# Two value passes a head instead of three, value halves moved into the attentions, and four tiles at once in an output projection

## Chip, cores and metric

The kernel runs on one core of one Trainium2 chip. The metric is the device time of one execution in microseconds; before the change three runs had a median of 1339.58 us (1339.01 to 1339.7).

## What is computed

Two transformer blocks over 512 tokens of width 1024, one after the other, in float32. Of the reference only the three attentions and what surrounds them matters here:

```
# block 1
h = rms_norm(x, mix_norm_g);  proj = h @ w_in
fq, fk, fv, flog, dq, dk, dv = split(proj)         # 512 columns each (flog: 8)
fox_out  = softmax(q k^T/8 + cumulated log gates, causal) v       # "fox": 8 heads of 64
diff_out = rms_norm((softmax(q1 k1^T/8 + alibi) - lam softmax(q2 k2^T/8 + alibi)) v)  # "diff": 4 heads, v is 128 wide
x = x + concat(fox_out, diff_out) @ w_out
x = x + (silu(h w_gate) * (h w_up)) @ w_down;  x = rms_norm(x)
# block 2
q, k, v, c_a, c_b, g_a, g_b = split(rms_norm(x) @ w_in_2 + b_in_2)
br_a = neighbourhood_attention(q, k, v, rpb) @ w_na_out           # "na": 8 heads of 64
br_b = silu(layer_norm(dwconv31(c_a * sigmoid(c_b)))) @ w_conv_out
x = x + (sigmoid(g_a) * br_a + sigmoid(g_b) * br_b) @ w_out_2
x = x + (gelu(gate) * val) @ w_down_2;  out = rms_norm(x)
```

## The kernel before, in words

**Precision.** Every operand is split into a high part (what the tensor engine's fp32r format keeps) and a low part (the rest). A product is three matmuls into one PSUM bank: high x high, high x low, low x high (`mm3`, L764 to L766).

**Weights.** They come in units of 128 x 1024 floats, numbered in the order of use by `plan_units`. SyncE loads unit u into one of two RAW buffers (L608) once GpSimd has made the low part of unit u-2. ScalarE converts RAW to the high part WH (`hi_part`, L1214; four slots, so it waits until unit u-4 is used), GpSimd subtracts to the low part WL (L736). `hi_next(u)` converts unit u+4 and stands in ScalarE's program where unit u has just been used. SyncE's list also holds the copies that put a head's rows in place (`head_rows`, L617 to L620); `HEADS_BEFORE` says ahead of which unit. They wait for ScalarE's split of that head (`head_part`, L1277 or L1279, semaphore head_hi).

**Attention.** Each of the three attentions is a list of 32 score tiles (128 queries against up to 512 keys), run in steps 0 to 36 that all engines walk through in the same order. In step i TensorE does: the scores of tile i (L945, L946); filler, which is chunks of projections taken from `fill_plan`; the value pass for the probabilities of tile i-4 (`pv_half`, for every second tile; for "diff" `pv`, once a head); the transposes of tile i-2 (L960). ScalarE does: the copy PTH of the transposed tile i-3 (L1361), the exponential of tile i (L1371), the scaling of tile i-1 (L1378), the copy of a finished head's output (L1401), then the splits of heads that `HEAD_STEPS` lists for this step, then `hi_next` for the filler that ends in this step. VectorE does: mask, minimum and negation of tile i (L1949), the reciprocal, low parts of heads (L1792, L1795), other work (`behind`: mask steps in "fox", taps of the convolution in "na", L2135), the low part PTL (L1983), the output's low part (L2001, L2004), and draining of the fillers. A value pass waits for PTL (ptl_done). In step 4h+8 head h's output is drained.

**Values.** `pv_half` uses as stationary operand the 128 value columns of a pair of heads (L764 to L766 with PTH, PTL) and takes half of the output rows. The four value tiles of each half of a projection (`v_tile`, `v_phase`, `v_parts`) are computed ahead of the attention: eight tiles ahead of "fox" (v1) and of "na" (v3). VectorE drains a tile with one scaling to T (L1746 with a bias row BVB, L1749), ScalarE copies T to VH, VectorE subtracts to VL (L1755).

**Output projection.** `half_units("out1", ...)` multiplies the "diff" half of the mixed heads. Its first two tiles take chunk k as soon as diff head k is ready (`mixed_ready`), the last of which is normalised and split after the last step (`diff_normed(3)`, `diff_low(3)`, L1908, L1913).

**Convolution.** `tap_plan` spreads 124 taps: 48 ahead of "na", 38 in its steps, 38 later.

Of the kernel before, what the change touches and what calls it, by code (L numbers as in the profile page):

```python
# [33 lines left out]
F32 = mybir.dt.float32  # L34
# [28 lines left out]
def plan_units():  # L63
# [28 lines left out]
    for j in range(4):  # L92
        u += col("w_in_2", NQ + P * j) + col("w_in_2", NK + P * j)
        if j == 0:
            u += v("w_in_2", NV)
# [40 lines left out]
def program(nc, d):  # L136
# [40 lines left out]
    def heads_memory(tag, o):  # L177
        return dict(VH=at("VH" + tag, o, [P, TC, S], F32R), VL=at("VL" + tag, o + 8192, [P, TC, S], F32R),
# [24 lines left out]
    BVB = at("BVB", BIG + 82432, [P, S], F32)  # L203
# [20 lines left out]
    CAUSAL = at("CAUSAL", BIG + 84480, [P, S], F32)  # L224
    NMB = tiny("NMB", [P, 2, S], BF16)
# [38 lines left out]
    def tap_plan():  # L264

        early = [(t, 0) for t in range(6)]
        for t in range(21):
            early += [(t, 1), (t + 6, 0)]
        during = []
        for t in range(4):  # L270
            during += [(t + 21, 1), (t, 2), (t + 27, 0), (t, 3)]
        for t in range(4, 10):
            during += [(t + 21, 1), (t, 2), (t, 3)]
        for t in range(10, 12):
            during += [(t, 2), (t, 3)]
# [26 lines left out]
    bv_in = sem("bv_in")  # L302
# [60 lines left out]
    o_free = sem("o_free")  # L363
    od_copy = sem("od_copy")
# [36 lines left out]
    for name, n in [("init", 8), ("fox0", 2), ("v1", 8), ("foxf", 8), ("v2", 4), ("difff", 18), ("out1", 8),  # L401
                    ("ffn1", 44), ("down1", 8), ("cab", 8), ("na0", 2), ("v3", 8), ("naf", 6), ("gates_b", 8),
# [4 lines left out]
    UN = {"fox0": 0, "v1": 2, "foxf": 6, "v2": 14, "difff": 16, "out1": 28, "ffn1": marks["ffn1"],  # L407
          "down1": marks["down1"], "cab": marks["down1"] + 24, "na0": marks["down1"] + 32,
          "v3": marks["down1"] + 34, "naf": marks["down1"] + 38, "gates_b": marks["gates"], "gates_a": marks["gates"] + 8,
          "na_out": marks["na_out"], "conv_out": marks["na_out"] + 4, "out2": marks["na_out"] + 8,  # L410
          "ffn2": marks["ffn2"], "down2": marks["down2"]}
    assert UN["out1"] + 4 == UN["ffn1"] and UN["naf"] + 6 == UN["gates_b"]
# [3 lines left out]
    for name in TL:  # L416
        PT0[name] = n_part
        n_part += {"init": 8, "v": 6, "v2": 3, "difff": 7, "out1": 4, "na_out": 4, "conv_out": 4}.get("v" if name in ("v1", "v3") else name, 0)


    per = {"init": (8, 8), "v1": (8, 8), "fox0": (0, 0), "foxf": (0, 0), "v2": (4, 4), "difff": (4, 0),
# [339 lines left out]
    def _(pe):  # L761
# [149 lines left out]
        for i in range(1, 4):  # L911
            v_tile("v1", i)
# [1437 lines left out]
```

## Time and profile before

| | before |
|---|---|
| median of 3 runs | 1339.58 us |
| profiled execution | 1337.46 us |
| its span (first to last instruction) | 1335.6 us |
| granted TensorE clock | 0.998 |
| POOL (GpSimd) busy | 670.1 us |
| ACT (ScalarE) busy | 639.8 us |

The page's busy time of PE (TensorE) counts a matmul from its start to its modelled end, and matmuls overlap. The distance between two starts tells what a matmul costs. A number in square brackets behind a row of an engine's order of time is the idle time before the instruction, and what ended it. An idle time on an engine other than the one that bounds costs nothing by itself.

### The profile page before, as it was taken

The numbers are of one execution on the slowest core, as the hardware profiler recorded it, in microseconds if no ns is written. First come the engines' busy times: TensorE is split into PE (matmuls) and PEld (weight loads), VectorE is DVE, ScalarE is ACT, GpSimd is POOL, SyncE is SP. The second block draws the span as 40 slices with busy tenths as digits, with TensorE's granted clock in tenths as the row PEclk, the third lists the DMA queues.
The fourth block names the chain that finished last, engine by engine and source line by source line (L and its number), as shares of the span: only waits on it lengthen the run. The fifth ranks groups of instructions, "written<-read, shape, count | busy, mean of one in ns | idle before, by whom it ended". The sixth has DMA issues, their size and how long they took to land.

```text
span 1335.6 us, 19126 instructions
## 1 busy us (share of the span) xinstructions
PE 1315.9 (99%) x6457; PEld 1104.4 (83%) x6457; DVE 657.5 (49%) x1237; ACT 639.8 (48%) x1015; POOL 670.1 (50%) x884
## 2 busy tenths in 40 slices
PE   9999999999999999999999999999999999999998
PEld 7988878788888888888888888888888888888887
DVE  7576586742222221112698884867445555551112
ACT  4488576754444333333436874464454444442222
POOL 7432343446555554555465344555655555554550
PEclk9999999999999999999999999999999999999999
DMA  6332332223333333333463332322333333333331
GB/s 181 99 85 72 80 111 80 64 79 111 101 102 95 94 102 93 92 103 92 93 144 92 82 82 77 94 95 80 110 93 97 100 101 97 94 90 101 89 99 63
DMA packets 220333, 127.22 MB, mean 95 GB/s; under 512 B 8642, under 2 KB 215887, under 8 KB 220143
## 3 DMA queue, kind: packets, MB, share of 16 engines
q1 hardware_dynamic: 220247, 126.39, 33.5%
q8 instruction: 37, 0.61, 0.2%
q14 instruction: 25, 0.20, 0.0%
q10 hardware_dynamic: 24, 0.01, 0.0%
HBM read 117.56 MB, written 2.47 MB: 90 GB/s over the span
## 4 chain that ended last, share of the span: by engine, by line
PE 90%; DVE 3%; ACT 3%; issue 2%; DMA 1%; POOL 1%; DVEq 0%; POOLq 0%; ACTq 0%
PE PS L764 28%; PE PS L766 28%; PE PS L765 28%; PE PS L960 1%; DMA RAW<-in_w_in 1%; PE PS L945 1%; PE PS L946 1%; ACT WH L1214 1%; POOL WL L736 1%; PE PS L841 0%; DVE PTL L1983 0%; DVE PS L2135 0%; PE PS L1159 0%; DVE PR L1949 0%; PE PS L867 0%
## 5 line engine op out<-in xcount | busy, mean ns | idle before, releaser
L736 POOL TENSOR_TENSOR WL<-RAW,WH 128x256 fp32r<-128x256 f32 x864 | 662.5, 798 | 635.3 <-ACT WH L1214 635.1
L1214 ACT ACTIVATE WH<-RAW 128x1024 fp32r<-128x1024 f32 (+1 forms) x220 | 228.8, 1042 | 436.0 <-PE PS L766 374.9
L764 PE MATMUL PS<-XH,WH 128*128 128x512 f32 x1072 | 419.1, 391 | 0.0
L765 PE MATMUL PS<-XL,WH 128*128 128x512 f32 x1072 | 417.8, 390 | 0.0
L766 PE MATMUL PS<-XH,WL 128*128 128x512 f32 x1072 | 417.8, 390 | 0.0
L766 PEld LDWEIGHTS PS<-XH,WL 128*128 128x128 f32 x1072 | 201.2, 188 | 42.7
L765 PEld LDWEIGHTS PS<-XL,WH 128*128 128x128 f32 x1072 | 201.3, 188 | 40.1 <-issue 0.7
L764 PEld LDWEIGHTS PS<-XH,WH 128*128 128x128 f32 x1072 | 201.3, 188 | 40.0 <-issue 0.7
L764 PE MATMUL PS<-HH,WH 128*128 128x512 f32 (+1 forms) x374 | 141.0, 377 | 0.0
L766 PE MATMUL PS<-HH,WL 128*128 128x512 f32 (+1 forms) x374 | 140.8, 377 | 0.0
L765 PE MATMUL PS<-HL,WH 128*128 128x512 f32 (+1 forms) x374 | 140.8, 377 | 0.0
L2071 DVE TENSOR_TENSOR T<-PS,R 128x512 f32<-128x512 f32 x44 | 30.3, 691 | 167.8 <-PE PS L766 158.2
L765 PEld LDWEIGHTS PS<-HL,WH 128*128 128x128 f32 x374 | 70.4, 188 | 13.0
L764 PEld LDWEIGHTS PS<-HH,WH 128*128 128x128 f32 x374 | 70.4, 188 | 13.0
L766 PEld LDWEIGHTS PS<-HH,WL 128*128 128x128 f32 x374 | 70.4, 188 | 12.7
L2263 DVE TENSOR_TENSOR T<-PS,R 128x512 f32<-128x512 f32 x44 | 30.4, 691 | 65.8 <-PE PS L766 56.2
L1371 ACT ACTIVATE PR<-PR,NM 128x384 f32<-128x384 f32 (+2 forms) x88 | 49.7, 565 | 26.7 <-DVE NM L1949 25.7
L764 PE MATMUL PS<-WH,XH 128*128 128x256 f32 x192 | 54.8, 285 | 1.2 <-DVE T L1746 1.2
L765 PE MATMUL PS<-WL,XH 128*128 128x256 f32 x192 | 54.3, 283 | 0.0
L766 PE MATMUL PS<-WH,XL 128*128 128x256 f32 x192 | 54.3, 283 | 0.0
L2094 DVE TENSOR_TENSOR X<-PS,X 128x512 f32<-128x512 f32 x8 | 5.5, 692 | 98.0 <-PE PS L766 98.0
L2135 DVE SCALAR_TENSOR_TENSOR PS<-U,VEC,PS 128x512 f32<-128x512 f32 x78 | 53.6, 748 | 0.1
(335 smaller groups left out, 1865.1 us busy)
## 6 DMA issues: line engine op xcount, KB each, us to landing
RAW<-in_w_up SPq DMA_DIRECT2D x66, 512.0 KB, 3.7
RAW<-in_w_in SPq DMA_DIRECT2D x60, 512.0 KB, 3.9
RAW<-in_w_down SPq DMA_DIRECT2D x32, 512.0 KB, 3.7
RAW<-in_w_gate SPq DMA_DIRECT2D x22, 512.0 KB, 3.7
RAW<-in_w_out SPq DMA_DIRECT2D x16, 512.0 KB, 3.6
RAW<-in_w_down SPq DMA_DIRECT2D x16, 384.0 KB, 3.2
QB<-QA SPq DMA_DIRECT2D x24, 128.0 KB
KA<-KA SPq DMA_DIRECT2D x24, 128.0 KB
```

What stands on the lines that cost most here:

```text
L736: ins = pool.tensor_tensor(WL[:, s, cs], RAW[:, s % 2, cs], WH[:, s, cs].bitcast(F32), ALU.subtract)
L764: pe.matmul(out, ah, bh, start=start, stop=False)
L765: pe.matmul(out, ah, bl, start=False, stop=False)
L766: return pe.matmul(out, al, bh, start=False, stop=stop)
L945: pe.matmul(out, mem["QA"][:, e, q], mem["KA"][:, e, ks], start=True, stop=False)
L946: pe.matmul(out, mem["QB"][:, e, q], mem["KB"][:, e, ks], start=False, stop=True).then_inc(sc_ready, 1)
L960: ins = pe.transpose(PS[:, TRB + g % 2, k * P:(k + 1) * P], probs[:, k * P:(k + 1) * P], IDF[:, :])
L1214: act.activation(WH[:, s, 0:width], RAW[:, s % 2, 0:width], ACT.Copy).then_inc(w_hi, 1)
L1371: act.activation(probs, probs, ACT.Exp, scale=-1.0, bias=NM[:, g % 4:g % 4 + 1], accum_out=RS[:, g % 4:g % 4 + 1]).then_inc(exp_ready, 1)
L2071: dve.tensor_tensor(T[:, s, 4:4 + S], src, R[:, :], ALU.mult).then_inc(acc_free, 1)
L2135: dve.scalar_tensor_tensor(out=homes[k], in0=src, scalar=w, in1=homes[before], op0=ALU.mult, op1=ALU.add).then_inc(conv_done, 1)
L2263: dve.tensor_tensor(T[:, s, 4:4 + S], src, R[:, :], ALU.mult).then_inc(acc_free, 1)
```

## The change

1. `pv_half`: the stationary operand is one head's 64 high and 64 low value columns side by side (V, a view of the memory of VH and VL), with two matmuls per key block (against PTH and PTL) instead of three. The result's two halves of 64 rows are added: ScalarE copies one (o_half), VectorE adds the other in PSUM (o_sum), for "na" with the bias, which makes the bias row BVB needless; then the output is copied and split as before. "diff" keeps its three matmuls.
2. Second value halves of "fox" and "na" become filler at steps 12 to 17 and 14 to 17; the Q tile of pair 1 of "fox" moves ahead of the attention; other fillers are respaced; the last value tile for "diff" becomes filler too. A value tile is now drained from PSUM by ScalarE (v_hi), then by VectorE (v_lo).
3. The unit order puts the second half of the values in front of the K tile of pair 3; the places of the head rows in the load list follow.
4. `tap_plan`: 40 taps ahead of "na", 46 within.
5. out1: two pairs of tiles run chunks 0 to 2 before the wait for diff head 3.

```diff
@@ plan_units
-    u += v("w_in", FOX_V)
+    u += v("w_in", FOX_V)[:2]
     for j in range(1, 4):
-        u += col("w_in", FOX_Q + P * j) + col("w_in", FOX_K + P * j)
+        u += col("w_in", FOX_Q + P * j)
+        if j == 3:
+            u += v("w_in", FOX_V)[2:]
+        u += col("w_in", FOX_K + P * j)
...
@@ units and fillers
-    UN = {"fox0": 0, "v1": 2, "foxf": 6, "v2": 14, "difff": 16, "out1": 28, "ffn1": marks["ffn1"],
+    UN = {"fox0": 0, "v1": 2, "foxf": 4, "v2": 14, "difff": 16, "out1": 28, "ffn1": marks["ffn1"],
...
-        qk_steps = [(0, 2), (3, 5)] + [(4 * f - 2, 4 * f + 1) for f in range(2, 8)]
         if kind == "fox":
-            for f in range(8):
-                add("qk", f, a + f, u + f, *qk_steps[f])
-            for i in range(3):
-                add("v", i, TL["v2"] + i, UN["v2"], N_SCORES + i, N_SCORES + i, False, PT0["v2"] + i + 1)
+            order = [("qk", 1, 0, 2), ("qk", 2, 3, 5), ("qk", 3, 6, 8), ("qk", 4, 9, 11), ("v", 0, 12, 13), ("v", 1, 14, 14),
+                     ("v", 2, 15, 16), ("v", 3, 17, 17), ("qk", 5, 18, 21), ("qk", 6, 22, 25), ("qk", 7, 26, 29)]
+            a, u = a + 1, u + 1
         elif kind == "na":
-            for f in range(6):
-                add("qk", f, a + f, u + f, *qk_steps[f])
-            for c in range(KD):
-                s0 = N_SCORES - 10 + 2 * c
-                add("gb", c, TL["gates_b"] + c, UN["gates_b"] + c, s0, min(s0 + 1, LAST_STEP))
+            order = [("qk", 0, 0, 2), ("qk", 1, 3, 5), ("qk", 2, 6, 8), ("qk", 3, 9, 11), ("qk", 4, 12, 13), ("v", 0, 14, 14),
+                     ("v", 1, 15, 15), ("v", 2, 16, 16), ("v", 3, 17, 17), ("qk", 5, 18, 20)]
...
+        if kind == "fox":
+            for i in range(TC):
+                add("v2", i, TL["v2"] + i, UN["v2"], N_SCORES - 2 + 2 * i, min(N_SCORES - 1 + 2 * i, LAST_STEP), i == 3,
+                    PT0["v2"] + i + 1)
+        elif kind == "na":
+            for c in range(KD):
+                s0 = N_SCORES - 11 + 2 * c
+                add("gb", c, TL["gates_b"] + c, UN["gates_b"] + c, s0, s0 + 1)
...
@@ SyncE's list
-    for kind, first in (("fox", UN["foxf"] + 6), ("diff", UN["difff"] + 6), ("na", UN["naf"] + 6)):
+    for kind, first in (("fox", UN["foxf"] + 7), ("diff", UN["difff"] + 6), ("na", UN["naf"] + 7)):
         for i, head in enumerate(range(2, 8)):
-            later = 1 if kind == "diff" else 0
+            later = 1 if kind == "diff" or kind == "na" and head >= 6 else 0
             HEADS_BEFORE.setdefault(first + i + later, []).append((kind, head))
...
@@ TensorE: pv_half
-                vc = slice((hd // 2) * P, (hd // 2) * P + P)
+                if half == 0 and hd == 4:
+                    pe.wait_ge(acc_free, late_values(kind))
+                values = mem["V"][:, :, hd, :, :].rearrange("p t a b -> p t (a b)")
...
                 for kc in kcs:
-                    ins = mm3(PS[:, OB + g % 2, q], mem["VH"][:, kc, vc], mem["VL"][:, kc, vc],
-                              mem["PTH"][:, kc, q], mem["PTL"][:, kc, q], kc == kcs[0], kc == kcs[-1])
+                    pe.matmul(PS[:, OB + g % 2, q], values[:, kc, :], mem["PTH"][:, kc, q], start=kc == kcs[0], stop=False)
+                    ins = pe.matmul(PS[:, OB + g % 2, q], values[:, kc, :], mem["PTL"][:, kc, q], start=False,
+                                    stop=kc == kcs[-1])
...
@@ TensorE: out1
+        pe.wait_ge(w_lo, UN["out1"] + 1)
+        for k in range(3):
+            mixed_ready(k)
+            out1_tiles([0], [k])
+        pe.wait_ge(w_lo, UN["out1"] + 2)
+        pe.wait_ge(acc_free, TL["out1"])
+        out1_tiles([1], range(3))
+        mixed_ready(3)
+        out1_tiles([0, 1], [3])
...
@@ ScalarE, VectorE: a head's output
+                if kind != "diff" and i - 5 in ready_after and ready_after[i - 5] % 4 == 3:
+                    hd = ready_after[i - 5] // 4
+                    own, other = half_rows(hd % 2), half_rows(1 - hd % 2)
+                    act.wait_ge(pv_ready, o0 + hd + 1)
+                    act.activation(o_temp(kind)[own, :], PS[other, OB + (o0 + hd) % 2, :], ACT.Copy).then_inc(o_half, 1)
...
+                    dve.wait_ge(o_half, f["o1"] + hd + 1)
+                    if kind == "fox":
+                        dve.tensor_tensor(bank[own, :], bank[own, :], o_temp(kind)[own, :], ALU.add).then_inc(o_sum, 1)
...
@@ ScalarE, ahead of "na"
-        v_parts("v3", M2, bias_columns)
+        act.wait_ge(rt_ready, 1)
+        for i in range(TC):
+            bias_columns(2 * i)
+            bias_columns(2 * i + 1)
+            v_hi("na", first_values("v3", i))
+        act.activation(LAM[:, 6:7], BT[:, :], ACT.Exp)
...
@@ VectorE, taps in "na"
-        attention("na", RP[:, :], lambda i: conv_taps(2 if N_SCORES - 8 <= i < N_SCORES else int(i % 4 != 3), n_during))
+        attention("na", RP[:, :], lambda i: conv_taps(2 if N_SCORES - 8 <= i <= N_SCORES else 1, n_during))
```

## Rows read from the trace of the kernel before

**Rows 1.** The page, busy us (share of the span) and instructions.
```profile
PE 1315.9 (99%) x6457; PEld 1104.4 (83%) x6457; DVE 657.5 (49%) x1237; ACT 639.8 (48%) x1015; POOL 670.1 (50%) x884
```

**Rows 2.** Stretches: length, busy us (instructions) PE, PEld, DVE, ACT, POOL; clock; DMA.
```profile
56.85:152.13 95.28, 92.84 (x578) 82.10 (x577) 61.57 (x180) 71.35 (x164) 30.42 (x40) 1.00 0.31 79
...
107.00:130.00 23.00, 23.00 (x142) 20.36 (x141) 13.43 (x44) 18.74 (x45) 6.69 (x10) 1.00 0.28 70
...
780.34:795.77 15.43, 15.43 (x87) 13.34 (x86) 14.27 (x29) 10.28 (x22) 7.26 (x8) 1.00 0.35 91
```

**Rows 3.** TensorE in order of time: start us, us; filler, then a value pass.
```profile
117.15 0.39 PE L766 MATMUL PS<-XH,WL 128*128 128x512 f32 x1
117.38 0.28 PE L764 MATMUL PS<-PTH,VH 128*128 128x256 f32 x1
117.50 0.28 PE L765 MATMUL PS<-PTL,VH 128*128 128x256 f32 x1
117.62 0.28 PE L766 MATMUL PS<-PTH,VL 128*128 128x256 f32 x1
```

**Rows 4.** TensorE in order of time, where it waited (and one transpose, 791.25).
```profile
68.58 0.55 PE L960 MATMUL PS<-IDF,PR 128*128 128x128 f32 x3 [0.74 <-ACT PR L1378]
...
76.99 0.39 PE L764 MATMUL PS<-PTH,VH 128*128 128x256 f32 x1 [0.70 <-DVE PTL L1983]
...
135.95 0.39 PE L764 MATMUL PS<-PTH,VH 128*128 128x256 f32 x1 [1.00 <-DVE PTL L1983]
...
170.91 0.36 PE L945 MATMUL PS<-KA,QA 128*128 128x256 f32 x1 [1.27 <-issue]
...
255.01 0.47 PE L764 MATMUL PS<-MH,WH 128*128 128x512 f32 x1 [1.98 <-DVE ML L1913]
...
696.49 0.36 PE L764 MATMUL PS<-WH,XH 128*128 128x256 f32 x1 [1.24 <-DVE T L1746]
...
734.95 0.39 PE L764 MATMUL PS<-PTH,VH 128*128 128x256 f32 x1 [1.07 <-DVE PTL L1983]
...
791.25 0.38 PE L960 MATMUL PS<-IDF,PR 128*128 128x128 f32 x2
```

**Rows 5.** ScalarE in order of time.
```profile
110.86 0.59 ACT L1401 ACTIVATE MH<-PS 64x512 fp32r<-64x512 f32 x1
...
114.87 1.04 ACT L1214 ACTIVATE WH<-RAW 128x1024 fp32r<-128x1024 f32 x1
115.82 0.57 ACT L1361 ACTIVATE PTH<-PS 128x512 fp32r<-128x512 f32 x1
...
696.37 0.53 ACT L1505 ACTIVATE BN<-BNR 128x384 f32<-128x384 f32 x1 [0.99 <-DVE T L1746]
696.80 0.40 ACT L1261 ACTIVATE VH<-T 128x256 fp32r<-128x256 f32 x1
...
789.49 1.06 ACT L1214 ACTIVATE WH<-RAW 128x1024 fp32r<-128x1024 f32 x1 [3.27 <-DMA RAW<-in_w_in]
```

**Rows 6.** VectorE in order of time; the last row is the page's, all taps.
```profile
111.49 0.69 DVE L2001 TENSOR_TENSOR ML<-PS,MH 64x512 fp32r<-64x512 f32 x1 [1.40 <-ACT MH L1401]
...
116.43 0.69 DVE L1983 TENSOR_TENSOR PTL<-PS,PTH 128x512 fp32r<-128x512 f32 x1
...
805.34 1.23 DVE L2135 SCALAR_TENSOR_TENSOR SQ<-U,VEC,SQ 128x512 f32<-128x512 f32 x1
...
L2135 DVE SCALAR_TENSOR_TENSOR PS<-U,VEC,PS 128x512 f32<-128x512 f32 x78 | 53.6, 748 | 0.1
```

**Rows 7.** SyncE's issues in order of time: start us, us, line, what.
```profile
116.43 0.57 SPq L608 DMA_DIRECT2D RAW<-in_w_in  x1
...
123.79 0.59 SPq L608 DMA_DIRECT2D RAW<-in_w_in  x1
...
168.52 0.60 SPq L620 DMA_DIRECT2D KA<-KA  x1
```

**Rows 8.** The page, DMA issues: count, KB each, us from issue to landing.
```profile
RAW<-in_w_in SPq DMA_DIRECT2D x60, 512.0 KB, 3.9
```

More of the change, by code:

```diff
@@ L494, in values_due, with values_place, values_shape, first_values @@
     def values_due(kind, step):
-        return [it for it in fill_plan(kind) if kind == "diff" and it["what"] == "v" and it["s1"] == step - 1]
+        return [it for it in fill_plan(kind) if it["what"] == "v" and it["s1"] == step - 1]
+    def values_place(kind, t, half):
+        mem = FAM[kind]["mem"]
+        if kind == "diff":
+            c = slice(256 * half, 256 * half + 256)
+            return mem["VH"][:, t, c], mem["VL"][:, t, c]
+        return tuple(mem["V"][:, t, 4 * half:4 * half + 4, j, :] for j in range(2))
+    def values_shape(kind, ap):
+        return ap if kind == "diff" else ap.rearrange("p (h c) -> p h c", c=HD)
+    def first_values(name, i):
+        return dict(what="first", idx=i, a=TL[name] + i, unit=UN[name], part=PT0[name] + i + 1)
+    def late_values(kind):
+        return max(it["a"] for it in fill_plan(kind) if it["what"] == "v") + 1
     def fill_chunks(it, step, n):
@@ L525, in keys_of, with o_temp @@
         return NA_KEYS[qb] if kind == "na" else (0, qb + 1)
+    def o_temp(kind):
+        return OTN if kind == "na" else ODR[:, 0, :]
     def pair_index(kind, hd):
@@ L537, in head_tiles @@
         if pair == 0:
-            a = {"fox": TL["fox0"], "diff": TL["foxf"] + 6, "na": TL["na0"]}[kind]
+            a = {"fox": TL["fox0"], "diff": TL["foxf"] + 10, "na": TL["na0"]}[kind]
             return a, a + 1
+        if kind == "fox" and pair == 1:
+            return TL["foxf"], TL["foxf"] + 1
         return tuple(it["a"] for it in fill_plan(kind) if it["what"] == "qk" and it["idx"] in (2 * pair - 2, 2 * pair - 1))
@@ L910, in _ @@
         ins.then_inc(fl_ps, 1)
-        for i in range(1, 4):
+        for i in range(1, TC):
             v_tile("v1", i)
@@ L920, in _ @@
         ins.then_inc(cum_ps, 1)
-        for i in range(4, 8):
-            v_tile("v1", i)
+        fm_tile(UN["foxf"] // 4, UN["foxf"] % 4, TL["foxf"])
         def attention(kind):
@@ L1128, in _ @@
         rt_transposes(RP)
-        for i in range(8):
+        for i in range(TC):
             v_tile("v3", i)
@@ L1307, in gate_logs @@
                     act.dma_start(dst, src).then_inc(head_in[head], 16)
-        v_parts("v1", M1, gate_logs)
+        act.wait_ge(rstd_tokens, 1)
+        for i in range(TC):
+            gate_logs(i)
+            v_hi("fox", first_values("v1", i))
+        gate_logs(TC)
+        act.activation(LAM[:, 6:7], BT[:, :], ACT.Exp)
+        hi_next(UN["foxf"])
         def gate_part(c):
@@ L1756, in v_low, with v_lo, v_phase @@
                               ALU.subtract).then_inc(low_done, 1)
-        def v_phase(name, mem, bias, extra):
-            slots_drained(name)
-            for i in range(8 + 1):
-                if i < 8:
-                    v_take(name, i, bias)
-                if i >= 1:
-                    v_low(name, i - 1, mem)
+        def v_lo(kind, it, name):
+            t, half = it["idx"], int(it["what"] == "v")
+            hi, lo = values_place(kind, t, half)
+            dve.wait_ge(act_done, H0[name] + t + 1)
+            dve.scalar_tensor_tensor(out=lo, in0=values_shape(kind, ps(it["a"], 256)), scalar=RT[:, t:t + 1],
+                                     in1=hi.bitcast(F32), op0=ALU.mult, op1=ALU.subtract).then_inc(acc_free, 1)
+        def v_phase(kind, name, extra):
+            for i in range(TC):
+                v_lo(kind, first_values(name, i), name)
                 extra(i)
+            extra(TC)
         def qk_take(name, i, r):
```

170 lines of the change are left out of this document (85 added, 85 removed).

## The prediction, made before the changed kernel was run

> **What bounds the kernel now.** I read the page first, then the busy times of each stage, then TensorE's own order of time, and last what the other engines do at the few places where TensorE stands still. TensorE is busy for 1315.9 of 1335.6 us, VectorE for 657.5 [rows 1]. The engine works through its matmuls in the order in which they are written, so there are only two ways to shorten this kernel: fewer matmuls, or fewer places at which one of them waits. The stage view and the engine's waits say where such places are: 2.4 us of the 95.3 of the first attention ("fox"), 1.2 in the third value projection, 1.1 and some small ones in the third attention ("na"), 2.0 before the output projection [rows 2, 4]. The last steps of "na" have no wait, but VectorE is busy for 14.27 of 15.43 us in four of them, so they have the least room [rows 2].
>
> A step is one score tile; three things then follow in each step: filler (projection chunks), the value pass of an earlier step, transposes. ScalarE and VectorE handle the softmax of the same steps, in an order that is also written out.
>
> **Part 1: two value passes instead of three.** The price of a matmul is the distance between two starts, not its listed duration, which overlaps the next one. Value matmuls of 256 columns start 0.12 us apart, though each is listed with 0.28; filler matmuls of 512 columns start 0.23 apart [rows 3]. Now the stationary operand holds a head's high and low half side by side (64+64 columns) instead of two heads' high halves, so high and low need one pass each over the two parts of the probabilities: 2 matmuls for 3. Per head there are 2+4 key blocks in "fox" and 3+3 in "na": 6 x 16 heads = 96 key blocks, so 96 matmuls go. "diff" keeps its three. 96 x 0.12 = **-11.5 us**, all of it on the engine that bounds. (The listed 0.282 each would give 27.1; that is the mistake to avoid.)
>
> The Trainium skill, "TensorE: Matmul & The Clock Gate", section "Wait — 56ns, not 53.3ns?", gives the spacing of warm matmuls as columns / 2.4 GHz plus about 2.5 ns. By that page the estimate is 109 ns at 256 columns and the saving 10.5 us; this trace has 120 ns at a granted clock of 1.00 (2.4 GHz) [rows 2, 3], and the trace decides.
>
> **Part 2: what each head gets in return.** The two halves must be added: ScalarE copies 64 rows from PSUM (0.59 by the nearest row, the copy of the head's output), VectorE adds them (0.69), and only then comes ScalarE's old copy [rows 5, 6]. ScalarE's old copy used to wait for VectorE's queue no longer than for its own; the new handoff runs parallel to ScalarE's exponential and scaling. 16 heads, 1.3 us each, none of it on TensorE. Around steps 20 to 28 ScalarE is busy for 18.74 of 23 us, 8.2 of each 10.08 that a head takes [rows 2]; one more copy makes that 8.8 of 9.4. I book nothing for it in "fox". In the last steps of "na" VectorE's 14.27 plus 0.7 stand against 15.43 - 0.72 for TensorE: 0.3 over, in each of two such stretches, **+0.7** [rows 2].
>
> **Part 3: second value halves as filler.** 4 tiles x 24 matmuls x 0.12 = 11.5 us leave the phase ahead of "fox" and the one ahead of "na" and come back inside; one Q tile (24 x 0.228 = 5.5) goes the other way. The sum on TensorE is zero. What can change is cover. Taken away: the stall of 0.74 (0.90 with the pipeline's refill) at 68.6, behind a late conversion, as units 8 and 9 no longer wait for the second value half; the 1.0 (1.17) at 135.95, as two steps that had no filler now have some; about half of the 0.70 (0.86) at 76.99 [rows 4]: **-2.5**. In "na" TensorE waits 1.07 at 734.95 and 1.1 in small pieces [rows 4]; steps get 0.5 to 1.2 us longer there and the extra convolution taps (0.75 each [rows 6]) take back a part: **-1.4**. Added: the first value tile ahead of "na" is now drained by ScalarE, then VectorE, and ScalarE does two bias columns (0.53 listed, 0.43 to the next start) before it. TensorE waited 1.24 there for VectorE's one operation; the chain is longer by 2 x 0.43 + 0.4 = **+1.2** [rows 4, 5]. The end of "fox" had value tiles of 2.9 us in steps 32 to 34; now 1.4 in each of 30 to 35, so the last value pass finds less ahead of it: between 0 and 2, I take **+1.2**, and 0.2 for the value tiles' own draining. The first scores of "fox" come six us sooner; their key rows are then issued at about 47.9 and, at the 2.4 us from a copy's issue at 168.52 to the scores that waited for it at 170.91 [rows 4, 7], are there at 50.3, before the 50.8 at which they are wanted: nothing.
>
> **Part 4: the output projection.** Before, two tiles run three chunks and wait for the fourth head: 1.98 idle, 2.14 with the refill [rows 4]. Three chunks of two more tiles (18 x 0.228 = 4.1 us) now stand there; their weights are made ready during "diff". Nothing else is late next: **-2.1**.
>
> **Part 5: what is moved in the load queue.** This decides. SyncE issues weights and the heads' rows in one list. The rows of a head wait for ScalarE's split of that head, and every weight load behind them waits too. Before, the fox heads' rows stood ahead of units 12 to 17, now ahead of units 11 to 16; but V[2:] was pushed in front of K3, so unit 15 is no longer the one converted at step 21 with a load issued five steps before: it is still converted at step 21 (four after K3, unit 11), and its load now stands behind head 6, which ScalarE splits in that very step. ScalarE comes to the conversion and waits; its queue is in order, so the probabilities behind it wait, and TensorE's value pass waits for those. In times of the trace before: head 6 split by 114.9, the load behind it issued at 116.43, 3.9 to landing [rows 8] = 120.3, conversion 0.95, transposed copy 0.5, VectorE's low part 0.7: 122.5. TensorE wants it at 117.38, less 0.24 saved since step 20: **+5.3**. Before, the conversion started at 114.87, at once, the low part ended at 117.1, and the pass had only 0.3 us to spare [rows 3, 5 to 7]. Head 7: rows ahead of unit 16, converted at step 25, one step after the split. The load behind its rows was issued at 123.79 [rows 7]; +3.9 + 0.95 + 0.5 + 0.7 = 129.8. TensorE's pass came a period of 10.08 after 117.38, at 127.5, less 0.5 saved in it: **+2.9**. Head 5: ahead of unit 14, converted two steps after the split. Two periods earlier than head 7 the load went out at 103.6, landed at 107.5; steps 16 and 17 now hold a half and a whole value tile (6.0 us instead of 4.7), so conversion, copy and low part end at 109.7 and the pass is due at some 108.6: **+1.1**. "na" has the like once: head 7 ahead of the fifth unit after, its conversion at step 24 instead of 25. Before, ScalarE stood still for 3.27 us there, until the landing at 789.49, and TensorE did not notice, as a whole step of work had gone ahead [rows 5]. Now that step is behind the wait, and the split itself waits for the new addition, behind two taps (up to 1.23 each [rows 6], so +2.4): landing at 791.9, then 0.95 + 0.4 + 0.6 + 0.6 = 794.4 for the scaled probabilities; the transposes that need them stood at 791.25, less 0.36 [rows 4]: 3.5. Without the delay of the split 1.1. I take **+3.0**.
>
> **Sum.** -11.5 - 2.5 - 1.4 - 2.1 = -17.5. Against it 5.3 + 2.9 + 1.1 + 3.0 + 1.2 + 1.2 + 0.2 + 0.7 = +15.6. Net -1.9 us on the profiled execution (1337.5, of which 1335.6 is the span), so 1335.6. The runs' median is 1339.6, 2.1 above the profiled one; I carry the difference over: **1337.7**. Unknown costs at their bounds: head 5 from 0 to 2, end of "fox" 0 to 2, "na" 1.1 to 4, start of "na" 0 to 2, gains inside "na" 0 to 2.3: about 1333 to 1342 for this case.
>
> **Rivals.** (B) The conversions do not hold the softmax up: the loads land earlier than I read, or the pipeline has more steps in hand than the 0.3 and 1.2 us I count. For it: in "na" a block of 3.27 us cost TensorE nothing [rows 5]. Against it: that one had a whole step ahead of it. Then 12.3 us of my debit fall away: 1325.4; half of it, 1331.5.
> (C) The ring of the new handoff, the slower side. Place: step 4h+8 of each head in "fox" and "na". ScalarE copies, VectorE adds, ScalarE copies again, VectorE subtracts; VectorE already stands 1.40 us in that step [rows 6]. If ScalarE has to wait for the addition before the next transposed copy, the bubble is up to 0.6 per head, 16 x 0.6 = 9.6: 1347. It decides from some 0.3 per head, 5 us, on. Against it: the addition (PTL's end, 0.4, plus 0.7) ends with ScalarE's exponential and scaling (1.0 to 1.1). The Trainium skill speaks for (C) in "na": "GPSIMD Engine Reference", section "1. Specifications", says that VectorE and GpSimd contend when VectorE has two SBUF inputs; the convolution taps do, eight more of them move into this attention, and here they take 0.75 on the mean and 1.23 at worst [rows 6].
> (D) The change does not do what it says for the time: the pass is a third shorter, but the pass before the next low part then stands waiting, and half of the 11.5 us turns up again as waits on PTL: 1337.7 + 5.8 = 1343.5. For it: three of the waits shown are on PTL; against it, they sum to 2.8 us only [rows 4], and the steps are not shorter but longer where value tiles and denser filler come in.
>
> **How the numbers follow.** My case 0.48, B 0.31, C 0.12, D 0.09. A measurement of this kernel can tell about 0.2% (2.7 us) from no change, so "same" is 1336.9 to 1342.3. My case falls 0.19 faster, 0.22 same, 0.07 slower, as its own width lies across the lower edge; B is 0.28 faster, 0.03 same; C 0.09 slower, 0.03 same; D 0.05 and 0.04. Together 0.47, 0.32, 0.21. The range takes in most of B and all of D: 1326 to 1344.
>
> **What would show it.** The value matmuls of L764's helper vanish for "fox" and "na" and 192 in two new lines stand there, 0.12 apart. ScalarE's conversion line waits on RAW for some 4 to 5.5 us once near step 21 of "fox", less near steps 18 and 25, and 5 us near step 24 of "na"; TensorE has as many waits on PTL or PR, 5 us the longest. No wait on ML before the output projection. If TensorE's longest wait in "fox" is under 2 us, part 5 is wrong and B holds; if its waits are many and alike, one per head, it is C.

## The result and the profile after

The change makes the kernel slower: 1347.44 us (median of 4, 1346.83 to 1348.34) against 1339.64 for the kernel before, measured beside it (4 runs, 1339.01 to 1341.02). The ratio is 1.0057, its 95% interval 1.004 to 1.0075: +7.8 us, where -1.9 was forecast, and above the stated range (1326 to 1344 us). The profiled execution's span went from 1335.6 to 1345.0, +9.4; the account below explains that difference.

The page of the kernel after: the busy times, the granted TensorE clock in 40 slices, and the weight loads with the median time from issue to landing.

```profile
PE 1311.0 (97%) x6361; PEld 1098.8 (82%) x6361; DVE 664.5 (49%) x1237; ACT 649.6 (48%) x1033; POOL 674.2 (50%) x884
...
PEclk9998899999999999999999999999999999999999
...
RAW<-in_w_in SPq DMA_DIRECT2D x60, 512.0 KB, 4.1
```

Against [rows 1] TensorE has 96 matmuls and 4.9 us of listed busy time less, and yet the span is longer. The fourth and fifth slices, in "fox", show a lower clock, where the kernel before has 9 in all 40. The five largest groups of TensorE's waits from the first scores on (engine, tile, line, releaser: us in total, times, longest):

```profile
PE PS L1010 <- DVE PTL L2047: 12.6, 5, 6.6
PE PS L995 <- ACT PR L1437: 4.4, 2, 4.2
PE PS L800 <- DVE V L1821: 3.6, 2, 2.9
PE PS L980 <- issue: 1.6, 1, 1.6
PE PS L995 <- DVE PTL L2047: 1.2, 1, 1.2
```

L1010 is the new value pass. Four of its five waits in order of time (start, duration, idle before it in brackets):

```profile
105.35 0.39 PE L1010 MATMUL PS<-PTH,V 128*128 128x256 f32 x1 [1.41 <-DVE PTL L2047]
121.57 0.58 PE L1010 MATMUL PS<-PTH,V 128*128 128x256 f32 x1 [6.64 <-DVE PTL L2047]
135.71 0.58 PE L1010 MATMUL PS<-PTH,V 128*128 128x256 f32 x1 [3.19 <-DVE PTL L2047]
155.70 0.39 PE L1010 MATMUL PS<-PTH,V 128*128 128x256 f32 x1 [0.87 <-DVE PTL L2047]
```

These are the places of the prediction's heads 5, 6 and 7 and the end of "fox". The wait on ML ahead of the output projection (1.98 in [rows 4]) is gone. The releaser of the long ones is not where they begin. SyncE's queue (L656 and L657 move a head's rows, L645 is the weight load behind them), and ScalarE's:

```profile
114.56 0.60 SPq L657 DMA_DIRECT2D KA<-KA  x1
115.58 0.38 SPq L645 DMA_DIRECT2D RAW<-in_w_in  x1
...
128.33 0.59 SPq L657 DMA_DIRECT2D KA<-KA  x1
128.97 1.33 SPq L645 DMA_DIRECT2D RAW<-in_w_in  x2
```

```profile
113.39 0.62 ACT L1338 ACTIVATE KA<-T 64x512 fp32r<-64x512 f32 x1
119.25 1.06 ACT L1272 ACTIVATE WH<-RAW 128x1024 fp32r<-128x1024 f32 x1 [5.24 <-DMA RAW<-in_w_in]
120.21 0.58 ACT L1420 ACTIVATE PTH<-PS 128x512 fp32r<-128x512 f32 x1
...
133.40 1.06 ACT L1272 ACTIVATE WH<-RAW 128x1024 fp32r<-128x1024 f32 x1 [4.19 <-DMA RAW<-in_w_in]
...
801.55 1.06 ACT L1272 ACTIVATE WH<-RAW 128x1024 fp32r<-128x1024 f32 x1 [5.35 <-DMA RAW<-in_w_in]
```

Read them as a chain: ScalarE ends the split of head 6 at 114.0, only then may SyncE move its rows and issue the load at 115.58; ScalarE meanwhile stands at the conversion L1272 for 5.24 us until it lands; the probabilities' copy (L1420) is queued behind it, and TensorE's value pass behind that. Something the prediction did not have is in the busy times of the same stretches (window: length, PE, PEld, DVE, ACT, POOL busy, then the granted clock):

```profile
103.56:114.54 10.98, 9.57 (x55) 8.06 (x54) 7.25 (x22) 8.60 (x21) 3.06 (x5) 1.00 0.01 3
114.54:121.50 6.96, 0.39 (x2) 0.00 (x0) 1.05 (x3) 2.25 (x5) 1.12 (x2) 0.73 0.43 115
121.50:132.10 10.60, 10.53 (x53) 9.39 (x54) 6.45 (x21) 7.00 (x17) 1.68 (x3) 0.86 0.25 61
132.10:135.70 3.60, 0.42 (x2) 0.00 (x0) 0.73 (x2) 2.31 (x5) 1.09 (x2) 0.87 0.71 185
135.70:144.00 8.30, 8.29 (x36) 7.36 (x37) 4.46 (x15) 6.29 (x16) 1.71 (x3) 0.64 0.01 3
803.80:810.00 6.20, 5.97 (x27) 5.18 (x28) 6.13 (x13) 4.22 (x11) 6.20 (x7) 0.73 0.30 85
```

The second and fourth are the stalls; behind them TensorE is busy all the time at a mean clock of 0.86 and 0.64, that is, partly at 1.2 instead of 2.4 GHz. There a filler matmul takes 0.43 us to the next start, where [rows 3] has 0.23:

```profile
138.44 0.63 PE L800 MATMUL PS<-XH,WH 128*128 128x512 f32 x1
138.87 0.63 PE L801 MATMUL PS<-XL,WH 128*128 128x512 f32 x1
139.30 0.63 PE L802 MATMUL PS<-XH,WL 128*128 128x512 f32 x1
```

**The account.** From TensorE's order of time, each matmul's distance to the next start is split in three: the usual distance for its width (0.109, 0.120, 0.175 and 0.227 us at 128, 256, 384 and 512 columns); what exceeds it where the next one waited ("stalls"); what exceeds it elsewhere ("slow"). Microseconds, before to after:

| stretch | matmuls | stalls | slow |
|---|---|---|---|
| ahead of fox | 50.6 to 44.5 | 1.4 to 1.4 | 2.8 to 2.6 |
| fox | 91.4 to 91.7 | 2.9 to 13.5 | 1.0 to 5.3 |
| diff to the start of na | 550.9 to 539.4 | 6.6 to 6.4 | 4.3 to 5.6 |
| na to the end | 609.4 to 615.3 | 5.1 to 8.9 | 2.5 to 3.7 |
| difference | -11.4 | +14.1 | +6.6 |

The sum is +9.3 of the +9.4. The matmuls are as forecast. The forecast's other terms made +9.6 of stalls and nothing slow. The growth of "slow" is the clock: of the 5.3 us in "fox", 4.25 fall where the trace grants half the clock (117.7 to 124.5 and 134.8 to 141.6), and the kernel before has no such stretch until its last 6 us.

### The profile page after: what moved, and what is told of

Its sections match the earlier page's. It is cut to its first block, busy times and chain, and to the rows that moved or that the text cites. A ratio compares the mean times of both kernels' runs of the same rounds, so it can differ in the third digit from the quotient of the medians.

```text
span 1345.0 us, 18926 instructions
## 1 busy us (share of the span) xinstructions
PE 1311.0 (97%) x6361; PEld 1098.8 (82%) x6361; DVE 664.5 (49%) x1237; ACT 649.6 (48%) x1033; POOL 674.2 (50%) x884
## 4 chain that ended last, share of the span: by engine, by line
PE 87%; DVE 6%; issue 2%; ACT 2%; DMA 2%; SPq 0%; POOL 0%; DVEq 0%; ACTq 0%; POOLq 0%
PE PS L800 27%; PE PS L801 27%; PE PS L802 27%; DMA RAW<-in_w_in 2%; DVE PS L2201 1%; PE PS L995 1%; PE PS L1010 1%; PE PS L980 1%; PE PS L981 1%; PE PS L1011 1%; DVE PTL L2047 1%; PE PS L877 0%; ACT PTH L1420 0%; DVE SQ L2201 0%; PE PS L1217 0%
## 5 line engine op out<-in xcount | busy, mean ns | idle before, releaser
L1272 ACT ACTIVATE WH<-RAW 128x1024 fp32r<-128x1024 f32 (+1 forms) x220 | 229.4, 1044 | 451.1 <-PE PS L802 368.8
L2341 DVE SCALAR_TENSOR_TENSOR PS<-T,VEC,PS 128x512 f32<-128x512 f32 x44 | 33.3, 756 | 41.3 <-ACT PS L1630 41.3
```

Source lines behind the costliest of these rows:

```text
L1272: act.activation(WH[:, s, 0:width], RAW[:, s % 2, 0:width], ACT.Copy).then_inc(w_hi, 1)
L2341: dve.scalar_tensor_tensor(out=z, in0=T[:, s, 3:3 + S], scalar=w(0), in1=z, op0=ALU.mult, op1=ALU.add).then_inc(cz_tap, 1)
```

## The experiments

"Repaired" below is the kernel after with both edits of the first two experiments. Each group of runs was measured beside the kernel before, whose median moved between groups from 1338.3 to 1339.8. Ratios are to that, with 95% intervals. A difference between two medians of different groups is therefore uncertain by some 1.5 us.

**One: the rows of "fox" a unit later.**

```diff
-    for kind, first in (("fox", UN["foxf"] + 7), ("diff", UN["difff"] + 6), ("na", UN["naf"] + 7)):
+    for kind, first in (("fox", UN["foxf"] + 8), ("diff", UN["difff"] + 6), ("na", UN["naf"] + 7)):
```

> The kernel after, with the rows of heads 2 to 7 of fox one unit later in the load queue (ahead of units 12 to 17 instead of 11 to 16); nothing else. Theory Q (a conversion on ScalarE is stuck behind a load that stands behind the rows of a head that was split just before): the three stalls of fox that follow a wait of ScalarE on RAW (1.57, 6.80 and 3.35 us over the pitch) go, 11.7 us, and with them the 4 us in which matmuls of fox ran at twice their distance after these stalls: 1347.4 - 15.7 = 1331.7. Rival H (the stalls come from the handoff's three more operations a head, and the load only fills a pause that is there anyway): ScalarE no longer waits on RAW, but TensorE still waits for PTL, at least 6 us in all: 1340 or more. Rival K (the slow matmuls are due to how dense the work is, not to the stalls): the stalls go, the 4 us stay: 1335.7.

Measured: 1333.68 us, ratio 0.9961 (0.9948 to 0.9974), 13.8 us under the kernel after. Stalls in "fox" fell from 13.5 to 3.7 us, slow matmuls from 5.3 to 1.3, and ScalarE has no wait on RAW left there. TensorE's waits:

```profile
PE PS L995 <- ACT PR L1437: 4.1, 2, 3.9
PE PS L1010 <- DVE PTL L2047: 2.5, 4, 1.0
```

The 3.9 is that of "na". Theory Q holds. H falls, as no 6 us of waits on PTL are left. The time alone lies midway between Q's 1331.7 and K's 1335.7; it is the trace that speaks against K, as the slow matmuls went with the stalls and no stretch of "fox" has a lower clock. But 2.5 us on PTL stay, in four pieces, one (0.6) at the place of the 6.64. The load was not the only thing late.

**Two: the rows of "na" heads 6 and 7 a unit later.**

```diff
-            later = 1 if kind == "diff" or kind == "na" and head >= 6 else 0
+            later = 1 if kind == "diff" else 2 if kind == "na" and head >= 6 else 0
```

> The kernel after, with the rows of heads 6 and 7 of na one unit later in the load queue, nothing else. Theory Q: the wait of ScalarE on RAW at 796 to 801 us goes, the stall of 4.40 us with it, and 1.7 us of slow matmuls behind it: 1347.4 - 6.1 = 1341.3. Rival (VectorE's eight added taps hold the probabilities up, and the load is only the last of two causes): a stall of 2 us or more stays at that place, behind VectorE or the split: 1344 or more.

Measured: 1339.88 us, ratio 1.001 (1.000 to 1.002), 7.6 under the kernel after. The stall of 4.4 is gone, and no wait over 0.5 us came in its place. In "na" that gave 3.2 us of stalls and 1.3 of slow matmuls. The other 3 us come from places that the edit does not touch: the third value projection waited 2.1 instead of 2.9 and had no slow matmuls behind it, and "fox" had 0.7 less of stalls and of slow matmuls. The expectation of 6.1 was right by luck in part.

**Three: the kernel before with only this edit.**

```diff
-    for kind, first in (("fox", UN["foxf"] + 6), ("diff", UN["difff"] + 6), ("na", UN["naf"] + 6)):
+    for kind, first in (("fox", UN["foxf"] + 5), ("diff", UN["difff"] + 6), ("na", UN["naf"] + 6)):
```

> The kernel before, with only the rows of heads 2 to 7 of fox one unit earlier in the load queue (ahead of units 11 to 16), as the change has them. Theory Q: this alone makes stalls behind conversions at steps 21 and 25 of fox, of some 5 and 3 us, with slow matmuls behind them of some 1.5 and 2.5 us: 1339.6 + 12 = 1351.6 (8 to 15 more). Head 5's stall (1.57 in the kernel after) needs the value tiles beside it and is smaller here. Rival H (the handoff or the filler is needed for the stalls): under 3 us, 1342 or less.

Measured: 1371.57 us, ratio 1.0239 (1.0225 to 1.0252): +32 us, over twice what was expected. In "fox" the stalls are 23.0 us longer than in the kernel before and the slow matmuls 6.9. The mechanism shows without handoff or filler, but for six heads, not two or three. ScalarE's conversions:

```profile
78.85 1.06 ACT L1214 ACTIVATE WH<-RAW 128x1024 fp32r<-128x1024 f32 x1 [5.46 <-DMA RAW<-in_w_in]
94.13 1.06 ACT L1214 ACTIVATE WH<-RAW 128x1024 fp32r<-128x1024 f32 x1 [4.75 <-DMA RAW<-in_w_in]
109.63 1.06 ACT L1214 ACTIVATE WH<-RAW 128x1024 fp32r<-128x1024 f32 x1 [5.41 <-DMA RAW<-in_w_in]
123.61 1.06 ACT L1214 ACTIVATE WH<-RAW 128x1024 fp32r<-128x1024 f32 x1 [3.51 <-DMA RAW<-in_w_in]
138.90 1.06 ACT L1214 ACTIVATE WH<-RAW 128x1024 fp32r<-128x1024 f32 x1 [5.21 <-DMA RAW<-in_w_in]
153.56 1.06 ACT L1214 ACTIVATE WH<-RAW 128x1024 fp32r<-128x1024 f32 x1 [3.99 <-DMA RAW<-in_w_in]
```

I had checked heads 6 and 7 alone. In the order of before, units 11 to 16 are converted at steps 5, 9, 13, 17, 21 and 25, and heads 2 to 7 are split at steps 5, 8, 13, 16, 21 and 24: each conversion is in the step of the split or one behind. The waits alternate accordingly, 5.2 to 5.5 and 3.5 to 4.8 us. The change puts two value units ahead of K3, which moves units 11 to 13 away from the splits, so that only heads 5 to 7 are hit. The prediction had put the blame on these value units; they are what spares heads 2 to 4.

**Four and five: is it the stall that lowers the clock?** Matmuls without a purpose fill the long waits of the kernel after.

```diff
+                if kind == "fox" and half == 1 and hd in (3, 4, 5):
+                    for _ in range({3: 10, 4: 50, 5: 24}[hd]):
+                        pe.matmul(PS[:, OB + g % 2, 256:512], mem["V"][:, 0, 0, :, :].rearrange("p a b -> p (a b)"),
+                                  mem["V"][:, 0, 0:2, :, :].rearrange("p h a b -> p (h a b)"), start=True, stop=True)
                 pe.wait_ge(ptl_done, t0 + 4 * hd + 2 * half + 2)
```

> The kernel after, with 84 more matmuls of 256 columns (10, 50 and 24) ahead of TensorE's waits for the second value half of heads 3, 4 and 5 of fox, which are its three long stalls; they write columns that the next value pass overwrites, and the results stay as they are. They take 1.2, 6.0 and 2.9 us of stalls of 1.57, 6.80 and 3.35. Theory C (the clock falls because TensorE stands still): the waits are as long as before in time, but the slow stretches behind them (4 us) go: 1347.4 - 4 = 1343.4. Rival K (the clock falls for another reason, the stretches stay): 1347.4 or a little more, as 84 matmuls are added.

Measured: 1346.69 us, ratio 1.0054 (1.0041 to 1.0067), 0.8 under the kernel after, not 4. Slow matmuls in "fox" fell from 5.3 to 2.9 us. The time is no clean test: in this run the load at head 6 took 5.0 us to land instead of 3.6, so a wait of 2.0 us stayed behind the 50, and behind it a clock of 0.84. So a second run had 12, 72 and 26.

> The kernel after with 12, 72 and 26 added matmuls of 256 columns (instead of 10, 50 and 24) ahead of the same three waits of fox, so that no stall over 2 us is left there. In the run with 84 of them a wait of 2.02 us stayed behind the second group, and 1.7 us of slow matmuls behind that; behind the third group neither. Theory C (the slow matmuls come after TensorE stands still for about 2 us or more, whatever was computed): none is left in fox (under 1.5 us over the whole of it; 5.3 in the kernel after), and the granted clock of every stretch of fox is 0.98 or more. Rival K: 1.5 us or more after step 24 stay without a wait ahead of them. The time itself: 1345 to 1348, as the added 13 us fill stalls of 12.

Measured: 1346.48 us, ratio 1.0057 (1.0042 to 1.0073). The whole of "fox", and the stretch behind the filled stall (124.6 to 136):

```profile
51.30:161.40 110.10, 107.32 (x712) 96.81 (x711) 68.05 (x189) 75.80 (x174) 31.02 (x41) 1.00 0.30 76
...
124.60:136.00 11.40, 11.40 (x72) 9.91 (x71) 5.67 (x16) 6.83 (x16) 0.79 (x2) 1.00 0.45 113
```

At the three places no wait over 0.6 us is left, the clock is 1.00 throughout, and slow matmuls are down to 1.8. That is above the 1.5 that theory C allowed, but none of it falls in a stretch with a lower clock, and the kernel before has 1.0 of the kind. The same conversions still come late; only TensorE was kept busy. So the slow stretches come from standing still, not from how dense the work is. The total did not fall, because 13.2 us of added matmuls took the place of 10.1 us of stalls and 3.6 of slow ones.

**Six: both repairs.**

> The kernel after with both repairs of the load queue (rows of fox one unit later; rows of heads 6 and 7 of na one unit later). If the two are independent: 1333.7 (fox rows alone) less the 7.5 that the na rows alone gave (1347.4 to 1339.9) = 1326.2, and 1.0% under the kernel before. Rival: the gain of the na rows held luck of the start of na (its third value projection waited 2.1 instead of 2.9 us there), then 1328.

Measured: 1328.29 us, ratio 0.9927 (0.9913 to 0.9941). The medians put it 5.4 under the first experiment, the ratios 4.6. That is as its rival had it: the gain of "na" alone is 4.5 (3.2 + 1.3), and the rest of experiment two's 7.6 was the spread in "fox" and the third value projection.

**Seven: the first value tile ahead of two bias columns.**

```diff
         for i in range(TC):
-            bias_columns(2 * i)
-            bias_columns(2 * i + 1)
+            if i:
+                bias_columns(2 * i)
+                bias_columns(2 * i + 1)
             v_hi("na", first_values("v3", i))
+            if i == 0:
+                bias_columns(0)
+                bias_columns(1)
```

> As the kernel with both repairs, and in the third value projection ScalarE takes the first value tile before its first two bias columns instead of after them. Theory: TensorE's wait for V there is shorter by the 0.85 us of two bias columns, and under 1.8 us it has no slow matmuls behind it: 1.0 to 2.3 less than the kernel with both repairs. Rival: the chain there hangs on VectorE's low halves of the first keys, not on ScalarE: no change.

Measured: 1327.07 us, ratio 0.9917 (0.9904 to 0.993). The wait for V went from 2.01 to 1.39 us, slow matmuls in that stretch from 1.6 to 0. The median fell by 1.2, which is in the expected span, but the two intervals overlap: the trace shows it, the times alone do not.

**Eight: the saved pass put back.**

```diff
+                    pe.matmul(PS[:, OB + g % 2, q], values[:, kc, :], mem["PTL"][:, kc, q], start=False, stop=False)
                     ins = pe.matmul(PS[:, OB + g % 2, q], values[:, kc, :], mem["PTL"][:, kc, q], start=False,
```

> As the kernel with both repairs, but each key block of fox and na has one matmul of 256 columns more (the value pass with the low part of the probabilities is done twice, so that this part is counted double in the output). 96 matmuls, 0.12 us each: theory P: 11.5 us more than the kernel with both repairs. Rival D (other engines take a part of the time back in either direction, as TensorE waits for PTL anyway): half of it, 5.8 or less.

The added matmul repeats the pass over PTL, so the low part of the probabilities counts double in the output; only the time is of interest. Measured: 1337.39 us, ratio 0.9985 (0.9976 to 0.9994), +9.1 on the repaired kernel. The usual distances of "fox" and of all that follows rise by 5.8 each, 11.5 in all. Stalls fall by 1.8 in "fox" and 1.7 in "na", and the third value projection waits 1.4 longer. TensorE's waits on PTL in the repaired kernel were 3.0 us in 6 at L1010 and 1.9 in 3 at L995; here:

```profile
PE PS L1010 <- DVE PTL L2048: 1.6, 2, 1.0
...
PE PS L995 <- DVE PTL L2048: 0.7, 1, 0.7
```

The price of 0.12 is right. The saving is worth about 8 net of what it turns into waits: rival D existed, at 3.5 us, not 5.8.

**Nine: the output projection as before** (two tiles through three chunks, then the wait; the banks as before).

> As the kernel with both repairs, but the first output projection takes two tiles at once, as the kernel before does. Theory: 1.98 us of wait on ML and 2.14 in all come back: 2.1 us more than the kernel with both repairs, 3.8 if matmuls are slow after that wait. Rival: VectorE is done with the fourth head sooner than before, and nothing comes back.

Measured: 1332.0 us, ratio 0.9949 (0.9936 to 0.9962), +3.7 on the repaired kernel. The wait comes back to the hundredth, and here slow matmuls follow it, 1.6 us, where the kernel before had none behind the very same wait. The stretch behind it in this kernel, then in the kernel before:

```profile
250.90:254.50 3.60, 3.50 (x10) 2.81 (x11) 1.88 (x3) 1.86 (x4) 2.80 (x4) 0.61 0.11 32
```

```profile
255.20:258.00 2.80, 2.80 (x13) 2.30 (x13) 1.91 (x3) 1.29 (x3) 2.75 (x4) 1.00 0.02 7
```

The third value projection also waited a microsecond longer in this execution, so the trace's +6.4 is not all due to the edit.

**Ten and eleven: what the handoff costs.** First the copy and the addition are left out, then the addition alone. A head's output then lacks the part of the low halves of the values (and its bias in "na"); these two kernels serve to find a cost.

```diff
-                    act.activation(o_temp(kind)[own, :], PS[other, OB + (o0 + hd) % 2, :], ACT.Copy).then_inc(o_half, 1)
...
-                        dve.tensor_tensor(bank[own, :], bank[own, :], o_temp(kind)[own, :], ALU.add).then_inc(o_sum, 1)
```

> As the kernel with both repairs (1328.3), but without the handoff of the two value halves: ScalarE's copy of 64 rows and VectorE's addition are left out for all 16 heads, so a head's output is the part of the high half of the values alone, without its bias in na. Theory (the handoff costs TensorE next to nothing, as the prediction has it: 0 in fox, 0.7 in na): 1327.6, and the PTL waits of 0.5 to 0.8 us in fox stay. Rival C (the handoff is what makes TensorE wait for PTL, 0.6 us a head at most): those waits go and it is 3 to 9 us faster.

Measured: 1322.54 us, ratio 0.9875 (0.9858 to 0.9891), 5.8 under the repaired kernel, 0.36 a head (7.0 by the ratios). Stalls fell from 3.7 to 1.2 in "fox" and from 4.5 to 1.3 in "na", and the waits on PTL all but vanish:

```profile
PE PS L1010 <- DVE PTL L2044: 0.9, 2, 0.5
```

> As the kernel with both repairs (1328.3; 1322.5 without the whole handoff), but only VectorE's addition is left out and ScalarE's copy of 64 rows stays, so a head's output lacks the low half of the values (and its bias in na). Theory V (VectorE's addition, with ScalarE's wait for it ahead of its second copy, is what costs): nearly all of the 5.8 us goes, 1323.5 or less. Rival S (ScalarE's 0.6 us copy ahead of the copy of the transposed probabilities costs): at most half of it goes, 1325.5 or more.

Measured: 1324.89 us, ratio 0.9892 (0.9875 to 0.9909), 3.4 under the repaired kernel. That lies between the two theories (1323.5, 1325.5), nearer to the rival. The traces say more. Without the whole handoff the stalls fall by 2.5 us in "fox" and 3.2 in "na", 5.7 together; without the addition alone by 1.7 and 2.9, together 4.6. The time shows less, because 1.7 us more of stalls came in this execution between "fox" and "na" (in the third value projection and at waits on WL), where the edit changes nothing. So VectorE's addition, with the wait for it, is the larger part of the cost and ScalarE's copy the smaller; times across these groups do not fix the shares.

**Twelve: the low part of a head's output one step later.** VectorE's order is changed, no work is taken away: its subtraction of L2072 and L2075 runs behind the next step's PTL instead of right behind the addition.

```diff
+                if kind != "diff" and i - 6 in ready_after and ready_after[i - 6] % 4 == 3:
+                    low_of(ready_after[i - 6] // 4)
...
-                    dve.wait_ge(oh_done, o0 + hd + 1)
...
+                    if i == LAST_STEP:
+                        low_of(hd)
```

> As the kernel with both repairs and the earlier value tile (1327.1), but VectorE takes the low part of a head's output one step later, behind that step's low part of the probabilities, so that it no longer stands 0.66 us in its queue waiting for ScalarE's second copy. Theory R (the ring of copy, addition, copy, subtraction keeps VectorE standing and with it the next row maximum): part of the handoff's 5.8 us comes back, 1 to 3 us faster. Rival: the standing time only takes the place of idle time that VectorE has anyway: 1327 within 0.7.

Measured: 1324.7 us, ratio 0.9892 (0.9875 to 0.9908), 2.4 under the kernel of experiment seven (3.3 by the ratios), where theory R had 1 to 3. In "fox" VectorE's standing for ScalarE's second copy, in the repaired kernel and then here:

```profile
DVE ML L2072 <- ACT MH L1460: 5.3, 8, 0.7
```

```profile
DVE ML L2005 <- ACT MH L1460: 0.7, 1, 0.7
```

In "na" the same standing falls from 5.3 to 0.7 too. But TensorE gained in "na" alone, where its stalls fell from 4.6 (experiment seven) to 2.2 us, while in "fox" they stayed at 3.7: there, this order gives TensorE nothing back.

This is the fastest version whose work is complete: 1.1% under the kernel before and 1.7% under the change as made.

## Why the prediction was wrong

**The clock was left out: the step that failed most.** No term of the sum, no rival and no bound held it. Between the forecast (-1.9) and the trace (+9.3) lie 11.2 us: 6.6 are this missing term, 3.8 are part 5's sizes, the rest is part 3 and small terms. Without either of the first two the time would have stayed inside the range. I booked a wait of 5 us at 5 us and never asked what TensorE does when it comes back, although the page prints the granted clock and it read 1.00 in [rows 2] because no wait of before was longer than 1.98 us. It cost 4.4 us in "fox", 1.3 at the third value projection and 1.2 in "na": 6.6 together with the small rest. Experiments four and five show by intervention that the waits cause it. With it the forecast would have been 1344.3, still 3.1 too low.

**Part 1 (-11.5)**: right. -11.4 in the trace, +11.5 for putting it back. What I did not follow is that a shorter pass brings TensorE earlier to the next wait: 3.5 of it comes back as waits.

**Part 2 (0 in "fox", +0.7 in "na")**: the second step that failed, as an argument. I compared busy sums with the period, found room and booked nothing. The handoff's cost is in its order, not in its length: ScalarE waits for VectorE's addition, VectorE then stands 0.7 us per head for ScalarE's copy, and VectorE's next operations stand behind that; experiment twelve shows that this last standing costs in "na" and not in "fox". Measured 5.8 in the repaired kernel. Rival C named this ring at 0.6 per head; it is 0.36, and it does decide from "some 5 us on", as stated there. In the kernel after it stands partly hidden behind the longer waits, so 5.8 is not added to the account above, and no run tells how much of it is there. Rival C's 1347 is the measured time by luck: its 9.6 us of bubbles, one a head, are not in the trace.

**Part 5 (+12.3)**: the mechanism is right at each of its four places, by the row and by experiments one to three; the sizes were low. Stalls: head 6 6.80 for 5.3, head 7 3.35 for 2.9, head 5 1.57 for 1.1, "na" head 7 4.40 for 3.0, in all 16.1 for 12.3. For head 6 the landing was no worse than I took (3.6 us after the issue at 115.58, for 3.9). What was off is the distance between the engines: I had the load's issue 0.7 us ahead of TensorE's arrival (116.43 against 117.14), it was 0.65 behind (115.58 against 121.57 - 6.64 = 114.93). TensorE had become faster in these steps by its shorter passes and ScalarE had not. I subtracted the one (0.24) and not the other. The traces split the loss by how long the split of head 6 ends before TensorE arrives at this pass. It is 2.42 us in the kernel before and 2.21 in experiment ten (rows repaired, no handoff), which is the shorter pass as forecast. It is 1.60 in experiment one (handoff, no late load): 0.6 for the handoff. It is 0.92 in the kernel after: another 0.7, which ScalarE had lost at the late conversion for head 5. The two make most of the 1.5 by which head 6 came out too small. The reason that part 5 gives for the overlap (the value units pushed in front of K3) is not the cause; experiment three has the stalls without them.

**Part 3**: in "fox" the old waits at 68.58 and 135.95 went as said, the one at 76.99 shrank by 0.16 only; the end of "fox" took 1.03 for 1.2. The third value projection took 1.6 more for 1.2, with a spread of its own: 1.24 and 2.18 us of wait in two traces of the kernel before and of experiment three, 1.75 to 3.42 in ten with the change and the bias columns ahead of the first value tile, 1.39 and 1.44 in the two (experiments seven and twelve) with the tile first. In "na" four old waits on PTL and the one at the end (2.74 us in all) went, but 2.3 came new: transposes for PTL (1.39) and a value tile for V (0.93). Both are gone without the handoff. So -0.4 for -1.4.

**The taps, which (C) and part 3 price at 0.75**, were misread. The last row of [rows 6] is not all taps but the 78 whose running sum lies in PSUM. Almost all of those inside "na" have it in SBUF and so read two inputs from there (kernel before; duration in ns shortest/median/longest, first and last start in us):

```profile
L2135 DVE SCALAR_TENSOR_TENSOR PS<-U,VEC,PS x78: 741/748/756, 656.3 to 867.7; 128x512 f32<-128x512 f32 x78
L2135 DVE SCALAR_TENSOR_TENSOR SQ<-U,VEC,SQ x14: 722/735/1341, 718.5 to 805.3; 128x512 f32<-128x512 f32 x14
```

There are 38 such taps before, 0.88 us on the mean, and 46 after, 0.93; all but two of them are in "na". In the kernel before they take 0.74 where GpSimd is idle (19 taps, 0.73 to 0.76) and 1.07 on the mean where it is busy all the while (13 taps, up to 1.34); the taps on PSUM take 0.75 in both cases. So the contention that (C) names is in these traces. It gives VectorE some 3.4 us more work than before, on top of the eight added taps (46 x 0.19 against 38 x 0.14). No run shows what of this reaches TensorE; with the rows moved, experiment two has no wait over 0.5 us in the last steps of "na", and the +0.7 booked there does not show.

**Part 4 (-2.1)**: right to the hundredth in the trace; worth 3.7 in the repaired kernel, as slow matmuls come with the wait there.

**What it would show** came as listed, with one difference: the conversion at step 25 waited 4.2 us, not clearly less than the 5.2 at step 21. B is excluded. C alone is excluded as well in the kernel after (few waits and uneven), yet it was what stood behind the stalls once these were taken away. I gave C and D 0.21 together and treated them as alternatives to my case; they were additions to it, all with the same sign. That is a second reason for a range that ended too low.

What stays open: why the wait in the third value projection differs between executions at all (1.75 to 3.42 us with the same order), how much of the handoff's cost is in the kernel after, and how it divides between the copy and the addition.

## What to carry to other kernels

Where an in-order DMA queue mixes weight loads with rows that wait for a compute engine, write down for every pair the step in which the rows become ready and the step in which the next load's data are wanted; equal steps cost nearly a full landing each here, and a reordering of the list elsewhere can create or remove six of them. Price a long wait of TensorE at its length plus the slow stretch behind it. When a pass gets shorter and a handoff is added beside it, follow each engine's arrival at the next meeting point instead of comparing busy sums, and try an operation that waits for another engine behind what the critical engine needs next (here worth 2.4 us of stalls in "na" and nothing in "fox").

## What the runs showed of the hardware that I had not expected

The clock's price, over all fourteen traces (the summed excess of the matmuls that run at 1.5 to 2.2 times their usual distance in the microseconds behind a wait of TensorE; start and end of the program left out). Behind 79 waits of 0.6 to 1.75 us there were never more than 0.54 us of such excess. Behind 19 waits of 1.98 to 3.45 us it was 0 to 0.3 in five cases and 1.1 to 2.5 in fourteen. Behind nine waits of 3.9 to 6.6 us it was 1.1 to 1.8 each time. So the same wait of 1.98 us before the output projection cost nothing in the kernel before and 1.6 us in two others: a wait of that size has to be priced at both values. The Trainium skill, "TensorE: Matmul & The Clock Gate", "Part 1: The HAM clock gate", says that the array runs at half rate after idling and at full rate after being busy again; the 0.43 us against 0.23 of the rows above agree.

A weight load of 512 KB at the same place of the queue took 3.6 us to land in one trace and 5.0 in another (the stall of head 6 in the kernel after and in experiment four), which moves a stall that hangs on it by as much.
